# Where the modulation panels stand in a shared weight ring: from fours in projections and branches to pairs in attentions and norms

## The chip, the cores and the metric

The kernel runs on 1 core of one Trainium2 chip. The metric is the device time of one execution in microseconds (us); lower is better. The engines have short names: PE (TensorE, matrix products), PEld (its weight loads), DVE (VectorE), ACT (ScalarE), POOL (GpSimd) and SP (SyncE, which issues the DMAs here).

## The reference

Two transformer blocks run one after the other on 256 tokens (the first also carries 256 context tokens), each with two layers, all in float32. The change touches only the first block:

```python
for l in range(DEPTH):                                    # DEPTH = 2
    mod_x = (silu(c) @ w_ada[l] + b_ada[l])               # 6 * 1024 columns
    mod_c = (silu(c_ctx) @ w_ada[l] + b_ada[l])
    sh1, sc1, g1, sh2, sc2, g2 = split(mod_x, 6)          # and the same of mod_c
    h = layer_norm(x) * (1 + sc1) + sh1
    p = h @ w_in[l]                                       # keys, values, queries, gates, Fourier input
    mix = gates * [fourier(..) @ w_fo, attend_m(..) @ w_mo, attend_g(..) @ w_go] @ w_o
    x = layer_norm(alpha * x + g1 * mix)
    h2 = layer_norm(x) * (1 + sc2) + sh2
    x = layer_norm(alpha * x + g2 * (relu(h2 @ w1) ** 2 @ w2))
```

The vectors c and c_ctx do not depend on the layers, so the product with `w_ada` (1024 x 6144 a layer, 48 MB in both) may be computed at any moment before its sixth is used.

## The kernel before

**One ring of weights.** Every weight reaches the chip as a panel of 1 MB (128 partitions x 2048 floats) in a ring of four slots. SP issues the loads in the order in which PE uses the panels. The load of panel n waits on `panel_begun` until the first matmul of panel n-3 is done, since from then on the slot of panel n-4 is free. So at most three panels are loaded or on their way while one is in use.

**Two kinds of panels.** A dense panel is split in two before use: ACT copies it with rounding into `ring_hi` (one instruction, L1466, in a function called `split`), and POOL subtracts that from the panel into `ring_lo`, which the profile calls `ring_r` (four instructions, L1446). PE waits for `lo_ready` of the slot (L751) and runs 48 matmuls (three products for each of 16 tile pairs; L783). A modulation panel (`w_ada`, 256 columns) isn't split: PE waits only for its landing. One call of `modulate()` on PE takes two such panels, a group: 2 x 8 matmuls against `silu_c` (the profile shows 32 records), then, for the group before, four small matmuls which turn its rows into columns (8 records, reading `hid_v` or `p_cmp`). ACT copies the rows out of PSUM (L1487), and DVE adds the bias (L2070). The 48 modulation panels are 24 groups; the first 4 groups stand ahead of everything, since layer 0 needs sh1 and sc1 at once.

**All orders are written by hand.** Each engine's program is a straight list, and each engine executes it in order. ACT's `split` of a dense panel stands in general two panels ahead of PE's use. Since POOL and the counters treated four slots as a unit, modulation panels stood in fours. The other 20 groups stand in layer 0: 4 in `project` (2 after its fourth dense panel and 2 at its end), 6 in the attention of kind m, 6 in that of kind g, and 4 in `branches` (2 after each of its two halves of six dense panels). Layer 1 has none.

**The norms.** `norm` sums x over its 1024 channels by 8 matmuls with ones, DVE centres, ACT squares, PE sums the squares, ACT takes the root, DVE the reciprocal and scales; in a norm with modulation ACT then applies scale and shift and rounds, and DVE makes the low part. After `mix_out` two norms follow each other, then the MLP's first panel; after the MLP one norm ends layer 0 and one opens layer 1.

**Attention.** A unit is one pair of heads on 128 queries. In step u PE computes the scores of unit u, then whatever else is placed there, then transposes the probabilities of unit u-1 (L810), then multiplies those of u-2 with the values. In kind m some steps also hold parts of the Fourier transform.

## Time and profile before

| What | Value |
|---|---|
| Median of three runs | 3257.94 us (3250.87 to 3266.14) |
| The profiled execution | 3254.99 us, its span 3253.2 us |
| PE busy | 2943.5 us, 90% of the span |
| First block and the start, 0 to about 1775 us | PE busy 1558.32 us |
| Second block, about 1775 us on | PE busy 1385.22 us of 1478.00 us |
| Granted TensorE clock, whole run | 0.947 |

PE leads in busy time everywhere, so the question for any stretch is what PE waits for in it, and what work PE does there that could stand elsewhere. In rows of the timeline the first number is the start in us, the second the duration, and the bracket at the end gives the idle time of the engine just before and what ended it.

### The profile page before, as it was taken

What the parts mean: (1) busy time and instruction counts of PE and PEld (TensorE: products, weight loads), DVE (VectorE), ACT (ScalarE), POOL (GpSimd) and SP (SyncE); (2) the same over time, 40 slices, a digit from 0 to 9 for tenths busy, and PEclk for the clock granted to TensorE, in tenths of its full rate; (3) what the DMA queues carried; (4) which work ended last, traced back from release to release, by engine and by line L of the source; (5) the groups of instructions that cost most, each with busy time, mean ns of one, the idle gap of its engine ahead of it and who ended that gap; (6) DMA issues with size and microseconds to landing.
All of it is one profiled execution on the core that took longest, in us unless ns stands there. A gap on an engine that the chain in (4) does not pass through costs nothing.

```text
span 3253.2 us, 49328 instructions
## 1 busy us (share of the span) xinstructions
PE 2943.5 (90%) x20273; PEld 2605.7 (80%) x20273; DVE 889.1 (27%) x1620; ACT 1244.7 (38%) x1672; POOL 1784.8 (55%) x1380
## 2 busy tenths in 40 slices
PE   5799888887999979889897999899998999899998
PEld 4576656674887847679897999889998998889998
DVE  1223233125112252333334212144211212144211
ACT  1423443223223233553443434454433434455432
POOL 1220214341545404247585887855887887756885
PEclk8889999989999989999999999999999999999999
DMA  7433325341322313135443556533454556534453
GB/s 222 116 92 112 95 98 156 122 129 30 100 90 91 97 32 91 53 104 156 130 170 128 161 176 169 169 117 117 156 182 156 169 180 171 169 104 130 156 181 117
DMA packets 397385, 422.60 MB, mean 130 GB/s; under 512 B 74550, under 2 KB 367406, under 8 KB 396919
## 3 DMA queue, kind: packets, MB, share of 16 engines
q1 hardware_dynamic: 397208, 420.06, 41.5%
q8 instruction: 134, 2.20, 0.3%
q14 instruction: 43, 0.35, 0.0%
HBM read 418.96 MB, written 3.16 MB: 130 GB/s over the span
## 4 chain that ended last, share of the span: by engine, by line
PE 82%; DVE 5%; POOL 5%; DMA 3%; ACT 3%; issue 2%; SPq 1%; DVEq 0%; POOLq 0%; ACTq 0%
PE ps L783 64%; PE ps L767 16%; POOL ring_r L1446 5%; PE ps L810 2%; ACT ring_hi L1466 1%; DVE arena L2092 1%; DMA ring<-in_w_in 1%; DVE stat L2205 1%; DMA ring<-in_w_ada 1%; DVE arena L2219 1%; DMA arena<-in_bucket_of_block 0%; PE ps L824 0%; DVE arena L2371 0%; DMA ring<-in_ffn_w_gate 0%; DMA ring<-in_w_branch_gla 0%
## 5 line engine op out<-in xcount | busy, mean ns | idle before, releaser
L1446 POOL TENSOR_TENSOR ring_r<-ring,ring_hi 128x512 fp32r<-128x512 f32 x1376 | 1784.6, 1333 | 1439.0 <-ACT ring_hi L1466 1437.0
L783 PE MATMUL ps<-hT_r,ring_hi 128*128 128x256 f32 (+1 forms) x6304 | 1178.7, 310 | 101.5 <-DVE hT_r L2384 36.6
L783 PEld LDWEIGHTS ps<-hT_r,ring_hi 128*128 128x128 f32 x6304 | 956.3, 197 | 169.3 <-issue 44.5
L1466 ACT ACTIVATE ring_hi<-ring 128x2048 fp32r<-128x2048 f32 x344 | 658.0, 1914 | 568.8 <-DMA ring<-in_ffn_w_down 136.3
L783 PE MATMUL ps<-hT_r,ring_r 128*128 128x256 f32 (+1 forms) x3152 | 712.6, 308 | 0.0
L783 PE MATMUL ps<-arena_r,ring_hi 128*128 128x256 f32 (+1 forms) x3792 | 641.8, 311 | 27.0 <-DVE arena_r L2293 9.5
L783 PEld LDWEIGHTS ps<-arena_r,ring_hi 128*128 128x128 f32 x3792 | 542.1, 190 | 74.1 <-issue 23.8
L783 PEld LDWEIGHTS ps<-hT_r,ring_r 128*128 128x128 f32 x3152 | 523.9, 196 | 24.7
L783 PE MATMUL ps<-arena_r,ring_r 128*128 128x256 f32 (+1 forms) x1896 | 358.4, 310 | 0.0
L783 PEld LDWEIGHTS ps<-arena_r,ring_r 128*128 128x128 f32 x1896 | 284.2, 190 | 20.8
L767 PE MATMUL ps<-arena 128*64 128x128 f32 (+9 forms) x1616 | 201.0, 366 | 24.6 <-DVE arena L2181 11.9
L767 PEld LDWEIGHTS ps<-arena 128*64 128x64 f32 (+4 forms) x1616 | 125.8, 174 | 70.4 <-issue 51.4
L2400 DVE TENSOR_TENSOR arena<-arena,ps 128x256 f32 (+1 forms) x88 | 33.1, 418 | 420.9 <-ACT arena L1812 420.9
L767 PE MATMUL ps<-arena,const 128*128 128x256 f32 (+3 forms) x348 | 105.3, 458 | 35.1 <-ACT arena L1494 17.1
L2350 DVE TENSOR_TENSOR arena_r<-arena,arena_r 128x512 fp32r<-128x512 f32 (+1 forms) x64 | 84.3, 1340 | 161.1 <-ACT arena_r L1755 161.1
L810 PE MATMUL ps<-const,arena 128*128 128x128 f32 x480 | 75.9, 307 | 53.8 <-DVE arena L2219 39.2
L767 PEld LDWEIGHTS ps<-arena,const 128*128 128x128 f32 (+2 forms) x348 | 66.1, 200 | 70.7 <-issue 47.4
L767 PE MATMUL ps<-ring_hi,hT_r 128*128 128x128 f32 (+2 forms) x640 | 114.6, 279 | 4.1 <-POOL ring_r L1446 2.5
L810 PEld LDWEIGHTS ps<-const,arena 128*128 128x128 f32 x480 | 63.1, 159 | 68.4 <-DVE arena L2219 50.7
L1632 ACT ACTIVATE arena<-ps,stat,rstd 128x512 f32<-128x512 f32 (+1 forms) x96 | 67.0, 702 | 123.3 <-DVE stat L2209 123.3
L1812 ACT ACTIVATE arena<-ps 128x256 f32<-128x256 f32 x88 | 29.1, 383 | 182.9 <-PE ps L783 182.9
L767 PEld LDWEIGHTS ps<-ring_hi,hT_r 128*128 128x128 f32 (+1 forms) x640 | 93.2, 175 | 6.0 <-POOL ring_r L1446 3.1
(215 smaller groups left out, 1954.7 us busy)
## 6 DMA issues: line engine op xcount, KB each, us to landing
ring<-in_w_in SPq DMA_DIRECT2D x82, 1024.0 KB
ring<-in_w SPq DMA_DIRECT2D x64, 1024.0 KB
ring<-in_w_ada SPq DMA_DIRECT2D x48, 1024.0 KB
ring<-in_ffn_w_up SPq DMA_DIRECT2D x44, 1024.0 KB
ring<-in_ffn_w_gate SPq DMA_DIRECT2D x44, 1024.0 KB
ring<-in_ffn_w_down SPq DMA_DIRECT2D x44, 1024.0 KB
ring<-in_w_in SPq DMA_DIRECT2D x48, 256.0 KB
ring<-in_w_o SPq DMA_DIRECT2D x8, 1024.0 KB
```

Of the source, the lines that this page charges most:

```text
L767: mm = pe.matmul(o, lhsT, rhs, start=start and j == 0, stop=stop and j == len(passes) - 1, skip_group_check=True)
L783: last[t] = pe.matmul(o, lhsT, rhs, start=start and j == 0, stop=stop and j == n - 1, skip_group_check=True)
L810: return pe.transpose(o, src, ident)
L1446: ins = pool.tensor_tensor(k.ring_lo[s][:, part], k.ring[s][:, part], k.ring_hi[s][:, part], ALU.subtract)
L1466: act.activation(k.ring_hi[s][:, :], k.ring[s][:, :], ACT.Copy).then_inc(k.hi_ready[s], 1)
L1632: act.activation(prob[:, buf, a, 0:n], ps[:, b, 0:n], ACT.Exp, bias=k.stat[:, 8 * buf + a:8 * buf + a + 1], scale=rstd_cq[:, tt:tt + 1] if ...
L1812: act.activation(area(SILU2, 2, 2, SEQ)[:, j % 2, m, :], ps[:, b, 0:SEQ], ACT.Silu).then_inc(k.bank_read[b], 1)
L2092: dve.reciprocal(std, std).then_inc(S["dve_step"], 1)
L2205: ins = dve.tensor_reduce(nmax[:, a:a + 1], ps[:, b, 0:n], AX, ALU.max, negate=True)
L2219: ins = dve.tensor_scalar(p, p, rsum[:, a:a + 1], None, ALU.mult)
L2350: dve.tensor_tensor(hid_lo[:, kt, :], hid[:, kt, :], hid_hi[:, kt % HID_SLOTS, :], ALU.subtract) \
L2400: dve.tensor_tensor(x[:, m, :], area(SILU2, 2, 2, SEQ)[:, j % 2, m, :], ps[:, b, 0:SEQ], ALU.mult) \
```

## The change

The change lets the two kinds of panels mix at any place of the ring. A string `RING` says of each panel of the first block whether it is a modulation panel (a) or dense (d). The counters of splits are kept for each slot, ACT's `split` skips modulation panels, and POOL's program, which was one loop, is written out for the first block. On that basis the 20 groups are placed anew: 6 in attention m of layer 0, 2 in attention g of layer 0, 3 in the norm after `mix_out`, 1 in the second norm, 3 in the norm after the MLP, 1 in the first norm of layer 1, 3 in attention m and 1 in attention g of layer 1. `project` and `branches` hold none. DVE adds the bias of groups in norms only after the norm. `mix_out` and the MLP of layer 0 no longer split the last two panels ahead; these splits now stand in the norm (one ahead of the scaling, one behind).

```diff
+RING = "a" * ADA_FIRST + "d" * 10 + "a" * 12 + "dddd" + "aa" + "dd" + "aa" + "d" * 16 + "a" * 8 + "d" * 32 + "a" * 8 \
+    + "d" * 10 + "a" * 6 + "dddd" + "aa" + "d" * 18 + "d" * 32
...
-QUADS_M, QUADS_G = (4, 6, 8, 10, 12, 14), (7, 8, 13, 14, 15, 16)
-AHEAD_M, AHEAD_G = (13, 15), (9, 10, 16, 17)
+MODS_M, MODS_G, MODS_LAST = ((4, 6, 8, 10, 12, 14), (2, 4, 6)), ((8, 13), (4,)), (14, 5)
+AHEAD_M, AHEAD_G = ((13, 15), (6, 7)), ((7, 9, 14, 15), (4, 5))
...
@@ SP: the order of the loads
-                    if c == 0 and l == 0:
-                        modulations(8, 4)
                 cols(416, 256)
-                if l == 0:
-                    modulations(12, 4)
...
-                if l == 0:
-                    modulations(16, 12)
+                modulations(*((8, 12) if l == 0 else (40, 6)))
                 for n in (0, 512):
                     gates(0, n)
-                if l == 0:
-                    modulations(28, 4)
+                modulations(20 if l == 0 else 46, 2)
                 for n in (0, 512):
                     out_of("w_fo", n)
                 if l == 0:
-                    modulations(32, 8)
+                    modulations(22, 2)
...
-                    if l == 0:
-                        modulations(40 + n // 128, 4)
                 for j in range(4):
                     s = slot()
                     load(s, [(at(s, 0, KD, 256), rows(W["w_o"][lay])[:, :, 256 * j:256 * j + 256])])
+                if l == 0:
+                    modulations(24, 8)
...
             mix_and_mlp(0)
+            modulations(32, 8)
             project(1)
...
@@ PE
-            def norm(cols, added):
+            def norm(cols, added, fill=(0, 0)):
...
                 mm.then_inc(k.bank_done[b], 1)
+                for _ in range(fill[0]):
+                    modulate()
                 sq = area(SQ, KD, TOK)
...
                 mm.then_inc(k.bank_done[b], 1)
+                for _ in range(fill[1]):
+                    modulate()
...
-                norm(slice(0, TOK), x_moved if l == 0 else None)
+                norm(slice(0, TOK), x_moved if l == 0 else None, (l, 0))
+                if l == 1:
+                    modulated_last()
...
-                norm(cols, last_results())
-                norm(cols, None)
+                fill = l == 0
+                norm(cols, last_results(), (1, 2) if fill else (0, 0))
+                norm(cols, None, (fill, 0))
+                if fill:
+                    modulated_last()
                 mlp(l, cols)
-                norm(cols, last_results())
+                norm(cols, last_results(), (1, 2) if fill else (0, 0))
...
@@ ACT
             def split():
 
+                while T.kind(1) == "a":
+                    T.whole_panel()
                 s, rounds, _ = T.panel()
...
+                for _ in range(fill[1]):
+                    modulate()
+                if last:
+                    modulated_last()
+                    split()
                 if affine:
```

Three places show how this moves instructions. First ACT in `project` of layer 0: the L1565/L1568 pairs take a query tile out of PSUM, L1466 is a split and L1487 the copy of a group's rows. Before:

```order
L1565 ACTIVATE arena<-ps 128x512
L1568 ACTIVATE arena<-ps,vecT 128x512
L1487 ACTIVATE hid_v<-ps 128x512
L1466 ACTIVATE ring0_hi<-ring0 128x2048
L1487 ACTIVATE p_cmp<-ps 128x512
L1466 ACTIVATE ring1_hi<-ring1 128x2048
L1565 ACTIVATE arena<-ps 128x512
```

The same place of the changed kernel (L1583/L1586 are the tiles, L1489 is the split):

```order
L1489 ACTIVATE ring1_hi<-ring1 128x2048
L1583 ACTIVATE arena<-ps 128x512
L1586 ACTIVATE arena<-ps,vecT 128x512
L1583 ACTIVATE arena<-ps 128x512
L1586 ACTIVATE arena<-ps,vecT 128x512
L1489 ACTIVATE ring2_hi<-ring2 128x2048
```

The copies of group rows are gone from between the query tiles, and each split stands ahead of the tiles before it.

Second, PE in the two norms after `mix_out` of layer 0. The changed kernel (xT,const are the sums of x, arena,const those of the squares, ring,silu_c one modulation panel, the 128x2 rows turn a group; before, only the four rows with 128x512 stood here):

```order
L774 MATMUL ps<-xT,const 128x512 x8
L774 MATMUL ps<-ring0,silu_c 32x256 x8
L774 MATMUL ps<-ring1,silu_c 32x256 x8
L774 MATMUL ps<-arena,const 128x512 x8
L774 MATMUL ps<-ring2,silu_c 32x256 x8
L774 MATMUL ps<-ring3,silu_c 32x256 x8
L774 MATMUL ps<-const,hid_v 128x2 x4
L774 MATMUL ps<-ring0,silu_c 32x256 x8
L774 MATMUL ps<-ring1,silu_c 32x256 x8
L774 MATMUL ps<-const,p_cmp 128x2 x4
L774 MATMUL ps<-xT,const 128x512 x8
L774 MATMUL ps<-ring2,silu_c 32x256 x8
```

One group now stands between the sums of x and of the squares, and two behind the squares, ahead of the next norm's sums.

Third, ACT from the second norm's root (L1498) to the MLP. Before (four splits stand in `mix_out`, ahead of the norms; the last two of them are those of the first two MLP panels):

```order
L1494 ACTIVATE arena<-arena 128x512 x8
L1498 ACTIVATE arena<-ps,const 128x512
L1505 ACTIVATE arena<-arena,mods 128x256 x4
L1510 ACTIVATE hT_r<-arena 128x512
...
L1505 ACTIVATE arena<-arena,mods 128x256 x2
L1510 ACTIVATE hT_r<-arena 128x512 x2
L1466 ACTIVATE ring2_hi<-ring2 128x2048
```

The changed kernel:

```order
L1518 ACTIVATE arena<-ps,const 128x512
L1489 ACTIVATE ring0_hi<-ring0 128x2048
L1530 ACTIVATE arena<-arena,mods 128x256 x4
L1535 ACTIVATE hT_r<-arena 128x512
...
L1535 ACTIVATE hT_r<-arena 128x512 x2
L1489 ACTIVATE ring1_hi<-ring1 128x2048
L1489 ACTIVATE ring2_hi<-ring2 128x2048
```

The splits of the MLP's first two panels (ring0, ring1) moved from ahead of the norms to one place between root and scaling and one behind the rounding. The first norm of layer 1 has the same form.

## Rows read from the trace of the kernel before

**Rows 1.** The page, part 1: busy time of each engine.

```profile
PE 2943.5 (90%) x20273; PEld 2605.7 (80%) x20273; DVE 889.1 (27%) x1620; ACT 1244.7 (38%) x1672; POOL 1784.8 (55%) x1380
```

**Rows 2.** Stretches: start:end, length, busy time by engine, granted clock, DMA share, GB/s.

```profile
140.10:157.70 17.60, 6.48 (x73) 3.79 (x73) 0.17 (x1) 6.84 (x8) 5.00 (x5) 0.67 0.90 238
187.50:197.30 9.80, 7.54 (x82) 4.70 (x81) 0.17 (x1) 2.10 (x3) 0.00 (x0) 0.82 0.88 275
197.30:212.90 15.60, 15.60 (x72) 13.19 (x72) 3.52 (x2) 4.56 (x5) 9.88 (x8) 0.61 0.42 98
598.90:614.70 15.80, 5.87 (x80) 3.61 (x80) 2.92 (x6) 6.23 (x5) 4.99 (x5) 0.75 0.81 265
614.70:683.60 68.90, 68.89 (x292) 55.95 (x295) 9.68 (x13) 11.18 (x12) 26.39 (x20) 0.96 0.31 92
683.60:702.20 18.60, 9.48 (x89) 6.45 (x89) 7.93 (x12) 9.36 (x9) 7.39 (x6) 0.64 0.70 226
748.70:797.50 48.80, 29.76 (x66) 12.32 (x64) 30.84 (x45) 15.84 (x27) 0.00 (x0) 0.93 0.00 0
```

**Rows 3.** Timeline of PE in layer 0's projection, around the first modulation groups.

```profile
140.03 2.80 PE L767 MATMUL ps<-ring,silu_c 128*32 128x256 f32 x48
146.15 1.94 PE L767 MATMUL ps<-ring,silu_c 128*32 128x256 f32 x16 [3.33 <-DMA ring<-in_w_ada]
...
157.68 2.07 PE L783 MATMUL ps<-hT_r,ring_hi 128*128 128x512 f32 x4 [7.80 <-POOL ring_r L1446]
```

**Rows 4.** The chain that ended last, same place: start, duration, what.

```profile
152.70 4.94 POOL ring_r L1446 x4
...
157.68 13.69 PE ps L783 x48
```

**Rows 5.** Timeline of PE in layer 0's attention g.

```profile
446.94 1.94 PE L767 MATMUL ps<-ring,silu_c 128*32 128x256 f32 x32
448.80 1.05 PE L767 MATMUL ps<-const,hid_v 128*128 128x2 f32 x8
...
454.56 1.09 PE L810 MATMUL ps<-const,arena 128*128 128x128 f32 x8 [2.56 <-DVE arena L2219]
...
462.21 2.07 PE L783 MATMUL ps<-arena_r,ring_hi 128*128 128x512 f32 x4 [4.91 <-POOL ring_r L1446]
...
511.14 1.93 PE L767 MATMUL ps<-ring,silu_c 128*32 128x256 f32 x32
...
530.45 2.07 PE L783 MATMUL ps<-hT_r,ring_hi 128*128 128x512 f32 x4 [4.57 <-POOL ring_r L1446]
```

**Rows 6.** Timeline of DVE between layer 0's branches and `mix_out`.

```profile
685.65 0.69 DVE L2283 TENSOR_TENSOR arena<-arena 128x512 f32<-128x512 f32 x1
...
699.84 2.24 DVE L2293 TENSOR_TENSOR arena_r<-arena,arena_r 128x1024 fp32r<-128x1024 f32 x1
```

**Rows 7.** Timelines of PE, ACT and POOL: layer 0's two norms and the MLP's start.

```profile
758.06 7.11 PE L767 MATMUL ps<-arena,const 128*128 128x512 f32 x16 [2.33 <-ACT arena L1494]
771.21 8.49 PE L767 MATMUL ps<-xT,const 128*128 128x512 f32 x16 [6.04 <-DVE xT L2106]
...
797.47 2.04 PE L783 MATMUL ps<-hT_r,ring_hi 128*128 128x512 f32 x4 [8.33 <-DVE hT_r L2100]
...
806.06 1.91 ACT L1466 ACTIVATE ring_hi<-ring 128x2048 fp32r<-128x2048 f32 x1
810.28 1.09 ACT L1745 ACTIVATE arena<-ps 128x512 f32<-128x512 f32 x2 [2.31 <-PE ps L783]
...
808.05 11.03 POOL L1446 TENSOR_TENSOR ring_r<-ring,ring_hi 128x512 fp32r<-128x512 f32 x8 [68.67 <-ACT ring_hi L1466]
```

**Rows 8.** Timeline of PE in layer 1's attention m, steps 4 and 6.

```profile
1333.52 2.86 PE L767 MATMUL ps<-const,arena 128*128 128x256 f32 x12
...
1350.44 1.09 PE L810 MATMUL ps<-const,arena 128*128 128x128 f32 x8 [0.64 <-DVE arena L2219]
```

**Rows 9.** The line L2283 of DVE, all of it: duration ns min/median/max, forms.

```profile
L2283 DVE TENSOR_TENSOR arena<-arena x32: 424/942/1229, 560.8 to 1511.0; 128x512 f32<-128x512 f32 x16, 128x256 f32<-128x256 f32 x16
```

More of the change, by code:

```diff
@@ L210, in whole_panel, with kind, split_rounds @@
         n = self.next("panel")
+        assert self.kind() == "a"
         slot = (self.count["panel"] - 1) % SLOTS
         return slot, self.value("panel", SLOTS - 1, SLOTS), n
-    def split_rounds(self):
-        return self.value("split", SLOTS - 1, SLOTS)
+    def kind(self, ahead=0):
+        j = self.count.get("panel", 0) - 1 + ahead
+        return RING[j] if j < PANELS_1 else "d"
+    def split_rounds(self, slot):
+        return self.value(f"split{slot}")
     @contextmanager
@@ L222, in loop @@
         tiles = per.pop("tiles", 0)
-        if "panel" in per and not per.pop("whole", False):
-            per["split"] = per["panel"]
+        for slot in range(SLOTS if "panel" in per else 0):
+            per[f"split{slot}"] = per["panel"] // SLOTS
         for j in range(tiles):
@@ L1476, in _ @@
             skip(KD)
-            def whole():
-                for _ in range(2):
-                    T.whole_panel()
             def modulation(group):
@@ L1495, in norm @@
                         .then_inc(S["squared"], 1)
+                for _ in range(fill[0]):
+                    modulate()
                 b, v = T.take()
@@ L1521, in modulate, with modulated_last @@
                 ada["turn"] = True
-            def whole_panels(quads):
-                for _ in range(2 * quads):
-                    whole()
+            def modulated_last():
+                skip(1)
+                ada["turn"] = False
             def project(l, cols):
@@ L1700, in branches @@
                         for j in range(3):
-                            last_two = l == 0 and g == 2 and j >= 1
-                            if not last_two:
-                                split()
+                            split()
                             if j == 2:
@@ L1773, in _ @@
                 halves, mod = (0, 1) if l == 0 else (1,), l * MODS
-                norm(plain, slice(0, TOK), modulated(mod + SC1, mod + SH1, (0, 1)))
+                fill = l == 0
+                norm(plain, slice(0, TOK), modulated(mod + SC1, mod + SH1, (0, 1)), (l, 0), not fill)
+                if l == 1:
+                    split()
                 project(l, cols)
@@ L2079, in scales, with norm @@
                 dve.wait_ge(S["dve_step"], T.next("dve_step"))
-            def norm(dst, cols, affine, ready):
+            def norm(dst, cols, affine, ready, fill=(0, 0), last=False):
                 n = cols.stop - cols.start
@@ L2088, in norm @@
                 dve.wait_ge(*k.moved(T.last()))
+                for _ in range(fill[0]):
+                    modulate()
                 for kt in range(KD):
                     dve.tensor_tensor(dst[:, kt, cols], k.xT[:, kt, cols], mean, ALU.subtract).then_inc(S["centred"], 1)
-                dve.wait_ge(*k.moved(skip(1)))
+                deviation = skip(1)
+                for _ in range(fill[1]):
+                    modulate()
+                if last:
+                    modulate(rows=False)
+                dve.wait_ge(*k.moved(deviation))
                 dve.reciprocal(std, std).then_inc(S["dve_step"], 1)
@@ L2308, in _ @@
                 if group >= 1:
-                    modulation(group - 1)
-            modulation(group)
+                    modulation(group - 1, *T.take())
+            modulation(group, *T.take())
             scales((SC1,))
@@ L2316, in _ @@
                 mod = l * MODS
-                norm(plain, slice(0, TOK), None, "h_ready")
+                fill = l == 0
+                norm(plain, slice(0, TOK), None, "h_ready", (l, 0), not fill)
                 project(l, cols)
@@ L2329, in _ @@
                 dve.wait_ge(*k.moved(T.last()))
-                norm(k.xT, cols, gained("ln1", l), "x_ready")
-                norm(plain, cols, None, "h_ready")
+                norm(k.xT, cols, gained("ln1", l), "x_ready", (1, 2) if fill else (0, 0))
+                norm(plain, cols, None, "h_ready", (fill, 0), fill)
+                if fill:
+                    scales((MODS + SC1,))
                 x = k.xT[:, :, cols]
```

166 lines of the change are left out of this document (70 added, 96 removed).

## The prediction, made before the changed kernel ran

> **What bounds the kernel now.** I read the page first, for the busy shares: PE 90%, POOL 55%, nothing else over 40% [rows 1]. PE also leads in every stretch that I cut with the windows. So a gain needs either less idle time of PE in layer 0 of the first block, or PE work moved from stretches where PE is full to stretches where it waits. Then I went through PE's timeline for idle times of a microsecond and more, and took the windows of the places where modulation groups stand [rows 2]. The reader is to see two things there. Where groups stand between dense panels, PE is busy for 6.48 us of 17.6, 7.54 of 9.8, 5.87 of 15.8 and 9.48 of 18.6. And the clock in them is 0.64 to 0.82, against 0.96 beside them. The reason is in the timeline: the first three panels of the four are there, the fourth is waited for (its load starts when the first is begun at 140.03 and it lands at 146.15, so a load takes 6.1 us when PE asks for it last), and the next dense panel, loaded later still, then needs its split and POOL's 4.94 us, so that PE starts again only at 157.68 [rows 3, 4]. Four light panels empty a ring of four, and the refill with the split is exposed.
>
> **The cost of a group.** 1.94 us for its two panels and 1.05 for turning the group before, 2.99 together at full clock [rows 5]; the 20 groups are 60 us of PE. A group that follows a finished series has none to turn and costs 1.94.
>
> **The cost of a restart.** A dense panel at full clock, p, and the loss of a restart, r: 13.69 = p + r [rows 4], and six panels with one restart take 68.9 = 6p + r [rows 2]. So p = 11.04, r = 2.65 us. The granted clock falls to the lower level (1.2 of 2.4 GHz) after waits like these, and the first matmuls after 157.68 take 2.07 us for four.
>
> **Gains, step by step.**
> (1) Projection of layer 0: the stretches of 17.6 and 9.8 us vanish, and one restart: 30.0. Nothing else waits there: p is twice POOL's 5 us for a panel and more than a load.
> (2) The sums that follow (197.3 to 212.9) ran at clock 0.61; 15.6 x 0.61 = 9.5 us at full clock [rows 2]. They came out of a group with waits; now they follow dense work, whose stretches have 0.96. Between 0 and 6.1; I take 5, since most of the sums' instructions are tiny and the clock may fall within them.
> (3) Attention g of layer 0. The wait of 4.91 us on POOL at 462.21 and its restart go (7.6), because the splits for w_fo stand in steps 7 and 9 and only two light panels precede. The removed groups themselves bring next to nothing: between scores and transposes PE waits 2.56 us anyway for DVE [rows 5], and a group fills that. At the end the last scores are at 511.14, and dense work starts at 530.45 [rows 5]. Without groups there the remaining steps are the 2.56 us wait, two pairs of transposes and three products with the values, at 1.1 us each, and one more step of ACT and DVE of about the length of that wait: 2.6 + 5.5 + 0.6 = 8.7, to about 519.8. That is 10.6 less, and the restart shrinks (2). Sum 20.2. Bounds: 7.6 if the end stays DMA-bound, 21.
> (4) Branches: the stretch of 15.8 us and its restart go (18.4). Behind the last branch panel 18.6 us become what the chain to `mix_out` needs: DVE's last sum ends at 686.34, 2.7 us after 683.6, ACT rounds (not longer than DVE's 2.24 for the same tile), DVE splits in 2.24 [rows 6]: 6 to 7, I take 6.2. Gain 12.4. Sum 30.9.
> Together 30.0 + 5 + 20.2 + 30.9 = 86.1 us.
>
> **Costs, step by step.**
> (5) The 8 groups in norms. The gap between the sums is 2.33 us [rows 7]: 1.94 fits, 2.99 costs 0.65. Two of the four have a group to turn: 1.3. The two groups behind the squares take 5.98 against a wait of 6.04 [rows 7], if their panels are there. The ring holds three when the norm begins; the fourth, fifth and sixth are loaded as the first, second and third are begun. The sixth is asked for at about 765.3 and is here at 771.4 by the 6.1 us above, so the next sums start near 772.4 and not at 771.21. They take 7.1 us at full clock but were stretched to 8.49 by DVE's pace, ending at 779.7: 772.4 + 7.1 = 779.5, no loss. Bounds 0 and, if loads under way together take twice 6.1, 6 us at each of the two places. I take 0.
> (6) The second split. Before, two panels were ready when the MLP began. Now the second is split behind ACT's rounding, from 806.06 + 0.65 on: ACT 1.91, POOL 11.03 / 2 = 5.5 [rows 7], ready at 814.1. The first panel is done at 810.28 + 0.65 (ACT reads it then). PE waits about 3.3 us, here and again at the projection of layer 1: 6.6. The third panel follows on POOL 5.5 us later, while PE needs 11, so it is not late.
> (7) The first split now has POOL at work while DVE scales the first tiles. DVE's additions from SBUF range from 0.42 to 1.23 us [rows 9], 0.69 for 512 columns with POOL at rest [rows 6]. Three such instructions lie on the way to the first h tile: 0 to 1.6 us at each of two places; I take 1 each, 2.
> The Trainium skill, "SBUF — State Buffer", section "Who interferes with whom", says that a DVE instruction with two SBUF inputs and a GpSimd one that reads SBUF share one port pair as an exclusive lock, held for a whole instruction. By that rule the place could cost one POOL instruction per DVE one, near the upper bound; the maximum of 1.23 agrees, as 0.69 and a part of a wait.
> (8) Layer 1's attentions take four groups. In m, step 2 has room; in step 4 the Fourier products of 2.86 us already fill the wait, so a group costs 2.9; in step 6 0.64 us is left, so 2.3 [rows 8]. In g 2.99 stands against 2.56: 0.4. Sum 5.6, bounds 1 and 12.
> Costs 1.3 + 6.6 + 2 + 5.6 = 15.5.
>
> **The sum.** The profiled execution took 3254.99 us, 3 us less than the median of 3257.94. 86.1 - 15.5 = 70.6 less gives 3184 against the profiled one, and 3187 for the median.
>
> **The rivals.**
> *Late refills in the norms.* PE's queue is in order: a group that waits for its panel holds the sums behind it, and these head the chain of the whole norm. For it speaks that eight panels are used in 30 us where 3 are in the ring. Against it: nothing else is loaded there (share 0.00 from 748.7 to 797.5), and the stretch of 17.6 us moved 238 GB/s, that is four panels [rows 2]. Each late panel costs up to 6.1; with 12 us at each of the two pairs of norms, and the second MLP panel later by the same slip, 30 us go back: 3217.
> *The bubbles move along.* The waits on POOL behind light panels could remain behind pairs, in attention g and at its end. Then of (3) only 7.6 is left or less and the layer 1 attention costs its 12: about 20 back, 3207. Against it: a pair leaves two dense panels in the ring, and their splits stand ahead.
> *More than summed.* Groups between the sums keep PE at work in the norms, so that the clock is still high when dense work comes, which now restarts at 797.47 with four matmuls in 2.04 us [rows 7]. Four restarts of 2.65 less would be 10.6: 3176. The Trainium skill, "TensorE: Matmul & The Clock Gate", Part 1, says that the throttled state is the default and activity releases it. Against it here: only one turn of 1.05 us falls into the last wait of 8.33.
> *Slower.* ACT's split in the norm stands ahead of the scaling. If the panel lands late, ACT holds h, and all behind it. Now nothing loads then, and this panel is asked for only when the sixth light panel is begun. It would have to be 36 us late at both places to eat 70.6 and 44 to be called slower; a load takes 6.1.
> *It doesn't do what it says.* POOL's program written out could run slower than the loop (its instructions must be fetched), and be the one PE waits for: POOL had 5 of 11 us to do, so it would have to double. Then the dense panels of layer 1, with half the tokens and so about p / 2, would be POOL's. That would leave 3230 to 3260.
>
> **How the numbers follow.** Chances: the forecast (3175 to 3200) 0.62, late refills 0.12, bubbles that move along 0.10, more than summed 0.10, POOL 0.04, slower 0.02. Range 3170 to 3218: from the third rival less some spread of runs (they differed by 15 us) to the first. A measurement of this kernel can tell about 0.5%, 16 us, from no change. Faster by over 0.5% holds all but the last two: 0.94; same 0.04, slower 0.02.
>
> **What would show it.** Projection of layer 0 without idle time of PE and about 30 us shorter; the sums behind it at a clock near 1; no L1446 wait in attention g; the branches in two times 66 us without a break and `mix_out` some 6 us behind. In the norms the 32x256 matmuls inside the old idle times, and the pair of norms with its start of dense work not over 3 us longer than its 48.8 [rows 2]. A wait of 3 us on POOL at the second panel of the MLP and of layer 1's projection. Layer 1's attention m some 5 us longer. I am wrong if PE waits on `w_ada` loads for more than 10 us in the norms, or if POOL's waits return in layer 1.

## The result and the profile after

The changed kernel takes 3208.67 us in the median of four runs (3207.76 to 3210.62), the kernel before 3260.78 us in four runs beside it (3250.87 to 3266.14). The ratio is 0.9844, with a 95% interval of 0.9819 to 0.987: faster by 1.6%, and 52.1 us less where the prediction had worked out 70.6. That is inside its range of 3170 to 3218, but outside the 3175 to 3200 to which it gave a chance of 0.62. The two profiled executions, which the stages below go by, have spans of 3253.2 and 3206.0 us: 47.2 less.

First the page of the changed kernel, part 1:

```profile
PE 2939.2 (92%) x20273; PEld 2603.9 (81%) x20273; DVE 899.4 (28%) x1620; ACT 1244.0 (39%) x1672; POOL 1780.7 (56%) x1380
```

PE works as long as before (2943.5 in [rows 1]), so nearly all that was gained is idle time. Where it went is read from windows cut at PE's own marks: the first dense panel of a stage, the first sums, the first scores. Of the kernel before, in the columns of [rows 2]: layer 0's projection, its attention g, the part of that up to the first `w_fo` panel, its end from the last scores beside a dense panel, the branches, the first half of the MLP, then layer 1's projection and attention m:

```profile
94.70:197.30 102.60, 89.22 (x513) 71.59 (x513) 10.92 (x18) 30.32 (x47) 19.94 (x16) 0.88 0.45 129
376.60:530.50 153.90, 128.38 (x879) 93.80 (x877) 50.84 (x124) 70.86 (x131) 27.26 (x21) 0.94 0.38 123
376.60:462.20 85.60, 71.16 (x418) 52.29 (x416) 25.96 (x73) 44.76 (x88) 15.16 (x12) 0.95 0.30 99
495.80:530.50 34.70, 26.20 (x310) 17.71 (x308) 15.46 (x32) 19.87 (x31) 7.11 (x5) 0.92 0.75 243
530.50:702.20 171.70, 152.65 (x744) 121.64 (x745) 35.81 (x44) 40.03 (x38) 69.21 (x50) 0.91 0.40 123
797.50:977.00 179.50, 176.12 (x769) 145.38 (x769) 31.15 (x47) 56.41 (x69) 81.48 (x64) 0.99 0.29 94
1206.90:1296.70 89.80, 82.52 (x506) 73.25 (x506) 30.41 (x48) 38.45 (x62) 40.85 (x32) 0.94 0.38 94
1296.70:1366.20 69.50, 60.13 (x380) 40.09 (x380) 25.51 (x56) 28.29 (x58) 10.11 (x8) 0.91 0.10 31
```

The same stretches of the changed kernel, with the sums behind the projection as its second row and the two norms as its seventh; these two answer to the rows 197.30 and 748.70 of [rows 2]:

```profile
97.30:169.50 72.20, 72.20 (x361) 61.41 (x362) 10.61 (x16) 30.67 (x44) 30.18 (x24) 0.98 0.37 88
169.50:182.50 13.00, 13.00 (x72) 11.56 (x70) 3.35 (x1) 1.97 (x3) 0.00 (x0) 0.73 0.00 1
344.50:496.60 152.10, 128.68 (x726) 94.56 (x724) 49.45 (x119) 65.08 (x124) 30.11 (x24) 0.87 0.21 70
344.50:430.30 85.80, 73.89 (x378) 52.98 (x376) 22.77 (x66) 43.66 (x83) 16.26 (x13) 0.89 0.23 74
463.90:496.60 32.70, 23.76 (x197) 17.96 (x195) 13.21 (x28) 14.25 (x25) 10.05 (x8) 0.74 0.20 65
496.60:634.10 137.50, 132.22 (x578) 108.11 (x577) 36.38 (x38) 39.65 (x34) 65.75 (x48) 1.00 0.32 92
681.50:735.90 54.40, 42.82 (x226) 20.87 (x224) 34.11 (x47) 19.84 (x31) 5.83 (x4) 0.87 0.49 155
735.90:922.90 187.00, 178.77 (x769) 147.00 (x769) 31.69 (x50) 58.28 (x70) 86.81 (x68) 0.97 0.28 90
1156.30:1250.80 94.50, 85.19 (x506) 74.92 (x506) 30.66 (x50) 40.42 (x63) 45.68 (x36) 0.92 0.36 89
1250.80:1326.60 75.80, 68.86 (x492) 46.56 (x492) 25.59 (x58) 29.78 (x61) 10.23 (x8) 0.87 0.35 112
```

The reader is to see: the projection is 30.4 us shorter and has no idle time left, the branches 34.2 shorter at a clock of 1.00. But attention g is only 1.8 us shorter, although it has four groups (some 12 us of PE) less to do and its wait on POOL ahead of `w_fo` is gone. Its clock fell from 0.94 to 0.87, to 0.74 at its end, and PE is busy for 128.68 us where it was for 128.38: 153 records fewer, in the same busy time. The costs stand in the norms (+5.6), the MLP (+7.5), layer 1's projection (+4.7) and its attention m (+6.3).

PE in attention g of the changed kernel. L817 transposes the probabilities, and the row of 477.96 holds the last scores:

```profile
426.60 1.09 PE L817 MATMUL ps<-const,arena 128*128 128x128 f32 x8 [2.63 <-DVE arena L2221]
...
476.06 1.97 PE L817 MATMUL ps<-const,arena 128*128 128x128 f32 x8 [1.55 <-DVE arena L2221]
...
477.96 2.77 PE L774 MATMUL ps<-arena 128*64 128x128 f32 x20
484.22 1.97 PE L817 MATMUL ps<-const,arena 128*128 128x128 f32 x8 [3.49 <-DVE arena L2221]
...
491.30 1.97 PE L817 MATMUL ps<-const,arena 128*128 128x128 f32 x8 [3.21 <-DVE arena L2221]
```

The same transposes (eight records) take 1.09 us and then 1.97, near the ratio of the two levels of the clock (2.4 and 1.2 GHz), and two of the three waits on DVE at the end are longer than the 2.56 us of [rows 5]. DVE in the same place (L2221 scales the probabilities, two tiles), and POOL's splits of the first two branch panels under it:

```profile
475.13 0.88 DVE L2221 TENSOR_SCALAR arena<-arena,stat 128x512 f32<-128x512 f32 x2
...
482.42 1.74 DVE L2221 TENSOR_SCALAR arena<-arena,stat 128x512 f32<-128x512 f32 x2
...
488.67 2.58 DVE L2221 TENSOR_SCALAR arena<-arena,stat 128x512 f32<-128x512 f32 x2
```

```profile
478.56 4.93 POOL L1456 TENSOR_TENSOR ring_r<-ring,ring_hi 128x512 fp32r<-128x512 f32 x4 [44.46 <-ACT ring_hi L1489]
485.85 5.12 POOL L1456 TENSOR_TENSOR ring_r<-ring,ring_hi 128x512 fp32r<-128x512 f32 x4 [2.37 <-ACT ring_hi L1489]
```

With POOL at rest the pair of L2221 takes 0.88 us, beside it 1.74 and 2.58.

Behind the projection PE is never idle, and yet the clock falls. These are the 64 products with one column, which end the sums, and the first dense products behind them:

```profile
172.06 10.54 PE L774 MATMUL ps<-const,arena 128*128 128x1 f32 x64
182.46 2.05 PE L790 MATMUL ps<-arena_r,ring_hi 128*128 128x512 f32 x4
```

The norms and the MLP's start on PE:

```profile
697.90 1.93 PE L774 MATMUL ps<-ring,silu_c 128*32 128x256 f32 x32
...
703.90 1.37 PE L774 MATMUL ps<-ring,silu_c 128*32 128x256 f32 x16 [2.07 <-DMA ring<-in_w_ada]
705.19 1.87 PE L774 MATMUL ps<-const,p_cmp 128*128 128x2 f32 x8
706.92 9.31 PE L774 MATMUL ps<-xT,const 128*128 128x512 f32 x16
...
735.88 2.04 PE L790 MATMUL ps<-hT_r,ring_hi 128*128 128x512 f32 x4 [9.03 <-DVE hT_r L2107]
...
753.21 2.08 PE L790 MATMUL ps<-hT_r,ring_hi 128*128 128x512 f32 x4 [4.85 <-POOL ring_r L1456]
```

The row of 697.90 begins the third modulation panel of the norms, at which the load of the sixth is asked for. The sixth is waited for (2.07 us), its group is followed by a turn at the lower clock (1.87 for 1.05), the sums take 9.31 where [rows 7] has 8.49, and the second MLP panel costs a wait of 4.85 on POOL and a restart (2.08 for its first four products). DVE's three scalings ahead of the MLP, beside the first split (POOL 728.66 to 734.49):

```profile
730.21 4.83 DVE L2104 TENSOR_TENSOR arena<-arena 128x512 f32<-128x512 f32 x3
...
735.65 0.69 DVE L2104 TENSOR_TENSOR arena<-arena 128x512 f32<-128x512 f32 x1
```

That is 1.61 us for one beside POOL, and 0.69 for one without.

### The profile page after: what moved, and what is told of

Same layout as the page of the kernel before. It is cut to its first block, busy times and chain, and to the rows that moved or that the text cites. A ratio compares the mean times of both kernels' runs of the same rounds, so it can differ in the third digit from the quotient of the medians.

```text
span 3206.0 us, 49208 instructions
## 1 busy us (share of the span) xinstructions
PE 2939.2 (92%) x20273; PEld 2603.9 (81%) x20273; DVE 899.4 (28%) x1620; ACT 1244.0 (39%) x1672; POOL 1780.7 (56%) x1380
## 4 chain that ended last, share of the span: by engine, by line
PE 83%; DVE 6%; POOL 4%; ACT 2%; DMA 2%; issue 2%; SPq 0%; DVEq 0%; POOLq 0%; ACTq 0%
PE ps L790 64%; PE ps L774 16%; POOL ring_r L1456 4%; PE ps L817 2%; DVE arena L2221 1%; DMA ring<-in_w_ada 1%; DVE stat L2207 1%; ACT ring_hi L1489 1%; DVE arena L2099 0%; ACT arena L1530 0%; PE ps L831 0%; DMA arena<-in_bucket_of_block 0%; DVE arena L2376 0%; DVE arena L2104 0%; DMA ring<-in_ffn_w_gate 0%
## 5 line engine op out<-in xcount | busy, mean ns | idle before, releaser
L1456 POOL TENSOR_TENSOR ring_r<-ring,ring_hi 128x512 fp32r<-128x512 f32 x1376 | 1780.5, 1331 | 1395.9 <-ACT ring_hi L1489 1394.9
L1489 ACT ACTIVATE ring_hi<-ring 128x2048 fp32r<-128x2048 f32 x344 | 657.8, 1914 | 502.8 <-DMA ring<-in_ffn_w_down 136.6
L774 PE MATMUL ps<-arena 128*64 128x128 f32 (+9 forms) x1616 | 205.8, 374 | 21.0 <-DVE arena L2184 11.9
L817 PE MATMUL ps<-const,arena 128*128 128x128 f32 x480 | 79.4, 316 | 63.4 <-DVE arena L2221 48.8
L817 PEld LDWEIGHTS ps<-const,arena 128*128 128x128 f32 x480 | 65.9, 164 | 76.9 <-DVE arena L2221 59.0
L774 PE MATMUL ps<-arena,const 128*128 128x256 f32 (+3 forms) x348 | 103.1, 451 | 24.7 <-ACT arena L1792 11.9
```

The source lines that it names most:

```text
L774: mm = pe.matmul(o, lhsT, rhs, start=start and j == 0, stop=stop and j == len(passes) - 1, skip_group_check=True)
L817: return pe.transpose(o, src, ident)
L1456: ins = pool.tensor_tensor(k.ring_lo[s][:, part], k.ring[s][:, part], k.ring_hi[s][:, part], ALU.subtract)
L1489: act.activation(k.ring_hi[s][:, :], k.ring[s][:, :], ACT.Copy).then_inc(k.hi_ready[s], 1)
```

## The experiments

The question was where 18 of the 20.2 us of term (3) went. *Theory A*: the waits that the removed groups no longer fill bring the clock to its lower level, and all work in and behind them takes longer. *Theory B*: the chain of scores, DVE, ACT and POOL sets the steps, and the clock only fills idle time. Others size the costs and rule out rivals. All kernels but `pool_written` are the changed one with the edit shown, and all ran five times or more beside the kernel before. The first four ran on one chip, where the kernel before stood at 3252.08 us (3250.62 to 3266.75, nine runs) and the changed one did not run. So a few us of their medians against 3208.67 are not certain, and their weight lies in the stages. The next four ran on one other chip, and one of them is the changed kernel again.

**Filler in three steps** (`g_filler`). Four products of constants that nothing reads, ahead of PE's wait for the probabilities:

```diff
+                            if a == 0 and l == 0 and kind == "g" and u in (14, 15, 16):
+                                for _ in range(4):
+                                    pe.matmul(ps[:, b, 0:256], ident, dft_d, start=True, stop=True, skip_group_check=True)
+                            if a == 0:
+                                pe.wait_ge(S["prob_ready"], T.next("prob_ready"))
```

> The changed kernel, with four matmuls of 256 columns without use ahead of the transposes in steps 14, 15 and 16 of layer 0's attention g, where PE waits for DVE. Theory A (the clock: the stretch from the last group of that attention to the branches took 29.7 us at a clock of 0.71, since the groups that used to fill PE's waits are gone): more PE work, yet the stretch gets 3 to 6 us shorter, clock over 0.85, median 3203 to 3206 against 3208.7. Theory B (POOL's splits slow DVE's L2221 from 0.88 to 1.74 and 2.58 us, and ACT's splits stand ahead of its copies): the stretch stays within 1 us of 29.7 or grows by up to 2.

Measured: 3212.48 us (3206.38 to 3215.37), ratio 0.9867 [0.9843, 0.9891], not faster than the changed kernel. The stretch from the last group to the branches is 26.9 us (466.6 to 493.5) for 29.7, at a clock of 0.87 for 0.71, and one of its three sets of transposes is still cold (at the lower clock, 1.97 us), behind a wait of 2.79. The clock is where theory A had it, the 2.8 us are just short of its 3 to 6, and the total does not show them. Alone it decided nothing: the clock was low in the steps ahead of these too.

**Splits one step earlier** (`g_early`).

```diff
-AHEAD_M, AHEAD_G = ((13, 15), (6, 7)), ((7, 9, 14, 15), (4, 5))
+AHEAD_M, AHEAD_G = ((13, 15), (6, 7)), ((7, 9, 13, 14), (4, 5))
```

> The changed kernel, with the splits of the branches' first two panels in steps 13 and 14 of layer 0's attention g, instead of 14 and 15. Theory B (POOL beside DVE): the last two L2221 pairs are back at 0.88 us for an instruction's pair as before, the stretch of 29.7 us gets 2 to 4 shorter, median 3205 to 3207. Theory A (clock): nothing or below 1 us, and the clock stays near 0.71.

Measured: 3210.41 us (3201.68 to 3212.38), ratio 0.9855 [0.983, 0.9879]. The same stretch takes 27.3 us at a clock of 0.81: the waits there are 3.40, 2.64 and 1.52 instead of 1.55, 3.49 and 3.21. The long ones moved one step forward with POOL's work. So POOL beside DVE is a part of the end, of about 2.4 us as theory B said, and the median does not show it.

**Both splits ahead of the scaling in the norms** (`two_splits`): ACT and POOL start the MLP's second panel before the h tiles, not behind them.

```diff
                 for _ in range(fill[1]):
                     modulate()
                 if last:
                     modulated_last()
                     split()
+                    split()
...
-                if l == 1:
-                    split()
...
-                if fill:
-                    split()
```

> The changed kernel, with both splits of the first two dense panels behind the norms standing together between root and scaling (before: one there, one behind the rounding), ahead of the MLP and of layer 1's projection. Theory: PE's waits of 4.85 and 2.02 us on POOL at the second panel and the restarts at the lower clock go: 4.85 + 2.65 and 2.02 + 2.65, less 0.5 each for ACT's second split ahead of the scaling: about 11 less, 3198. Rival: POOL then works beside DVE's scaling twice as long (DVE's three scalings took 4.84 beside POOL and 1.90 without), the first dense matmul comes 2 to 4 us later at both places, and the gain is 3 to 6: 3203 to 3206.

Measured: 3203.22 us (3200.77 to 3206.75), ratio 0.9844 [0.9821, 0.9866]; by the ratio no better than the changed kernel, by the median 5.5 us under it. The first half of the MLP takes 181.5 us for 187.0, layer 1's projection 91.7 for 94.5: 8.3 us of the 12.2 that the second split cost are back in these stages. But the norms ahead of them grew, from 54.4 to 55.3 us and from 52.6 (55.2 when the changed kernel ran again) to 56.7, since POOL's work on both panels now lies under the scaling. That is what the rival said, and its 3203 to 3206 came, not the 3198 of the theory. DVE:

```profile
725.08 4.84 DVE L2101 TENSOR_TENSOR arena<-arena 128x512 f32<-128x512 f32 x3
729.93 1.67 DVE L2104 TENSOR_TENSOR hT_r<-arena,hT_r 128x512 fp32r<-128x512 f32 x1
731.52 1.76 DVE L2101 TENSOR_TENSOR arena<-arena 128x512 f32<-128x512 f32 x1
```

**The norms' groups as one, one, one** (`norm_spread`) in place of one, two, none, so that no place needs four panels at once.

```diff
-                norm(cols, last_results(), (1, 2) if fill else (0, 0))
-                norm(cols, None, (fill, 0))
+                norm(cols, last_results(), (1, 1) if fill else (0, 0))
+                norm(cols, None, (fill, fill))
```

> The changed kernel, with the groups in norms as 1 between the sums and 1 behind the squares in each of the four norms, instead of 1 and 2, then 1 and 0. Theory of the late refill: the waits of 2.07 and 1.95 us for the sixth panel go, and the slow sums behind them (9.31 and 8.73 us instead of 8.5): the pairs of norms take 51 and 50.5 instead of 54.2 and 52.5, 5 us less: 3204. If the group in the last wait (9.03 us) also keeps the clock up, the first dense panel starts at full clock, 2.65 less at each place: 3199. Rival: the dense panels are now asked for later, the second split waits for its panel, and PE's wait behind the first dense panel grows by what the norms gain: 3208.

Measured: 3205.5 us (3203.18 to 3208.27), ratio 0.9846 [0.9823, 0.9869]. No wait for a panel is left in the norms. The second norm's sums start 13.15 us after the first norm's squares, as in the kernel before, where the changed kernel has 16.05, and they take 8.80 us for 9.31: 3.4 us less. But the two norms take 52.2 us for 54.4, only 2.2 less, and the pair that ends layer 0 takes 52.9 for 52.6. ACT copies the third group's rows ahead of its split, so that POOL comes last at the first dense panel, and this still starts at the lower clock:

```profile
731.17 2.07 PE L790 MATMUL ps<-hT_r,ring_hi 128*128 128x512 f32 x4 [7.29 <-POOL ring_r L1456]
```

So the group that stood in front of the sums was 3.4 us of the 5.6, and its new place gives 1.2 of them back. Of the two further parts of the expectation neither came: the group in the last wait did not keep the clock up, and the wait behind the first dense panel became shorter (3.90 us for 4.85), not longer.

**The changed kernel again** (`after_again`), without an edit.

> The changed kernel unaltered, so that the four kernels of this call have it on their own chip. If what I ascribe to the clock's phase is right, the same instructions take different times: attention g of layer 0 took 152.09, 146.55 and 152.14 us in three kernels that have it unaltered, and the norms that end layer 0 took 52.6, 56.7 and 52.9. I expect one of those values, the stages of dense work alone (branches 137.5, MLP's second half 180.8) within 0.3 us of before, and a median of 3205 to 3212.

Measured: 3208.43 us (3207.28 to 3215.14), ratio 0.985 [0.9835, 0.9864]. Attention g took 146.7 us in its profile, not 152.1; attention m 133.6 for 130.8, the norms that end layer 0 55.2 for 52.6; the branches 137.5 in both. The stretch from the last group to the branches is the same to 0.1 us, so the difference in attention g lies ahead of it. Here is its window, to be held against 344.50:496.60 above:

```profile
348.90:495.60 146.70, 122.92 (x726) 91.40 (x724) 49.27 (x119) 64.85 (x124) 30.17 (x24) 0.90 0.22 72
```

The same 726 records take 5.8 us less of PE at 0.90 than at 0.87. In stretches with waits the clock differs from run to run; in the branches it does not, and in the dense projection of layer 0 little (72.2 and 72.9 us). This is why one profile's stage is good to about 5 us there and to 0.1 in the branches.

**Filler in every waiting step of attention g** (`g_full`).

```diff
-                            if a == 0 and l == 0 and kind == "g" and u in (14, 15, 16):
+                            if a == 0 and l == 0 and kind == "g" and u in (1, 3, 5, 7, 9, 11, 14, 15, 16):
```

> Four unused 128x256 products stand ahead of PE's wait for the probabilities in every step of layer 0's attention g that waits (1, 3, 5, 7, 9, 11, 14, 15, 16), about 1.7 us each at full clock in waits of 1.8 to 2.6 us. Theory A (the lost 18 us of term 3 are mostly a lower clock, which the waits bring): the clock of the stage goes from 0.87 to 0.97 or more, the dense panels in it to 11.2 from 11.9 and 12.6, transposes to 1.07, the stage from 152 to 141 to 145 us, the whole to 3199 to 3203. Theory B (the chain through ACT, DVE and POOL sets the steps and the clock only fills their idle time): the stage stays at 149 to 154, the whole at 3207 to 3212.

Measured: 3201.32 us (3200.55 to 3202.67), ratio 0.9828 [0.9813, 0.9842], 7.1 us less than the changed kernel beside it, with no range in common. The stage, its part up to the `w_fo` panel, and its end:

```profile
342.00:480.80 138.80, 130.71 (x798) 97.73 (x796) 51.77 (x119) 64.64 (x124) 30.57 (x24) 0.99 0.24 76
342.00:420.30 78.30, 74.70 (x419) 55.65 (x417) 22.85 (x66) 42.74 (x82) 15.32 (x13) 1.00 0.25 81
451.60:480.80 29.20, 25.35 (x221) 18.57 (x219) 14.67 (x28) 14.17 (x25) 10.24 (x8) 0.94 0.23 73
```

The stage is 13.3 us shorter than in the changed kernel's first profile and 7.9 shorter than in its second, with 72 records more to do. The part up to `w_fo` takes 78.3 us for 85.8: 7.3 under the kernel before, where the prediction's first part of term (3) said 7.6. (The part held two groups before and holds one now, so the two numbers are near in part by luck.) Theory A holds, B falls for this part: PE is idle for 3.6 us of it where it was for 11.9, and its clock is 1.00 for 0.89. The four products take 2.0 us, not 1.7. Beside it stands what the Trainium skill says ("TensorE: Matmul & The Clock Gate", Part 1): the throttled state is the default and activity releases the throttle. By that rule work of no use can make a kernel faster, and this trace agrees: 0.87 without the products, 0.99 with them.

**The three placements together** (`three`): `g_early`, `two_splits` and `norm_spread`.

> Three edits together: the splits of attention g in steps 13 and 14 in place of 14 and 15, both splits of the norms ahead of the scaling, and the groups in the norms as one, one and one in place of one, two and none. If their effects by stages are real and add (attention g -6 to -8, MLP and projection of layer 1 -8.3, norms -2.2), the median is 3190 to 3195. If only what the medians showed adds (+1.7, -5.5 and -3.2), it is 3200 to 3204, and the difference is the phase of the clock, which an edit shifts at will.

Measured: 3197.42 us (3194.43 to 3201.44), ratio 0.9813 [0.9799, 0.9828]; 11.0 under the changed kernel beside it. Between the two forecasts (3190 to 3195, 3200 to 3204): the medians of the three alone add to 7.0 (-5.5, -3.2 and +1.7), the stages in the expectation to 16.5 and more. The stages do not simply add: the norms take 54.9 and 56.2 us here, so that the 2.2 us that the spread groups gained there do not show beside the two splits, and attention g takes 149.6.

**POOL written out in the kernel before** (`pool_written`): its loop unrolled for 24 rounds of four panels (`low` is the old body of the loop), all else as it was.

```diff
-            with pool.Fori(0, (PANELS_1 - ADA + LAYERS * PANELS_2) // SLOTS) as i:
+            written = 24
+            for i in range(written):
                 for s in range(SLOTS):
...
+                    low(s, i + 1)
+            with pool.Fori(0, (PANELS_1 - ADA + LAYERS * PANELS_2) // SLOTS - written) as i:
+                for s in range(SLOTS):
+                    low(s, i + 1 + written)
```

> The kernel before, with POOL's loop written out for its first 96 panels and looped for the rest, all else as before. Tests my rival that the written-out program is slower by itself. Theory: it costs nothing, as POOL has 5 of 11 us to do: the median of the kernel before within 5 us, POOL's four instructions for a panel 4.94 us as before. Rival: instruction fetch makes POOL late, with new waits on it in projection and branches, over 3265 us.

Measured: 3259.19 us (3251.15 to 3266.68, 12 runs) against 3257.72; ratio 1.0002 [0.9989, 1.0014]. POOL's line over the whole run, this kernel and then the kernel before (count, busy time, mean ns, idle time by releaser):

```profile
L1445 POOL TENSOR_TENSOR ring_r<-ring,ring_hi 128x512 fp32r<-128x512 f32 x1376 | 1784.0, 1330 | 1448.1 <-ACT ring_hi L1473 1446.5
```

```profile
L1446 POOL TENSOR_TENSOR ring_r<-ring,ring_hi 128x512 fp32r<-128x512 f32 x1376 | 1784.6, 1333 | 1439.0 <-ACT ring_hi L1466 1437.0
```

The rival that a written-out program runs slower falls. PE's program is that of the kernel before, so this profile is also a second one of it, and its attention g takes 159.0 us where the first has 153.9 (attention m 129.8 for 131.8).

**Placements and filler** (`three_full`): `three` with the products of `g_full`. This run and the next ran on a third chip, with the kernel before at 3258.4 us.

> The three edits of the run before together with the four unused products ahead of every waiting step of layer 0's attention g. If the products' gain of 7 us is the clock's and independent of where the splits stand, attention g falls from 149.6 to 138 to 141 us and the median from 3197 to 3188 to 3192. If the edits share one gain (the splits in steps 13 and 14 were already part of it), the median stays at 3194 to 3198.

Measured: 3193.08 us (3190.67 to 3199.54), ratio 0.9805 [0.979, 0.982]. Attention g takes 137.2 us, just under the 138 to 141 of the first theory, but the median lies between the two forecasts (3188 to 3192, 3194 to 3198). It is 4.3 below that of `three`, which ran on another chip, and the ranges of the two overlap. At the end no transposes are cold any more, and PE (L1051 is the filler) goes from the end of the last scores (469.61 + 2.15, in one row with the products ahead of them) to the branches in 10.2 us. From the last group (457.51) on it is 24.5 us at a clock of 1.00, 5.2 less than the 29.7 of the changed kernel, and `g_filler` and `g_early` had 2.8 and 2.4:

```profile
469.61 2.15 PE L774 MATMUL ps<-arena 128*64 128x128 f32 x20
471.70 1.99 PE L1051 MATMUL ps<-const 128*128 128x256 f32 x8
475.23 1.09 PE L817 MATMUL ps<-const,arena 128*128 128x128 f32 x8 [1.54 <-DVE arena L2222]
...
479.11 1.04 PE L817 MATMUL ps<-const,arena 128*128 128x128 f32 x8
...
481.97 1.19 PE L790 MATMUL ps<-hT_r,ring_hi 128*128 128x512 f32 x4
```

**Filler in the other attentions too** (`fill_more`): the same products in `u in {"m0": (13, 15, 16), "g0": ..., "m1": (7, 8), "g1": (5, 7)}`.

> As the run beside it, and the same four products also in the waits of the other attentions: steps 13, 15, 16 of m in layer 0 (waits 2.63, 2.63, 3.38), steps 7 and 8 of m in layer 1 (2.84, 2.85, transposes at 1.97) and steps 5 and 7 of g in layer 1 (4.51, 2.56). If the clock is what a wait costs beyond itself everywhere, attention m of layer 0 loses 2 to 4 us, that of layer 1 3 to 5, attention g of layer 1 1 to 3: the median is 6 to 10 us below the run beside it, 3180 to 3185. Rival: the products stand in the way in places where the wait is shorter than they are, and the median is within 3 us of the run beside it.

Measured: 3184.52 us (3182.28 to 3186.29), ratio 0.9772 [0.9759, 0.9785], 8.6 below `three_full` beside it, as the theory said (6 to 10), with no range in common, and 24 below the changed kernel on another chip: the best version here. Attention m of layer 0, then m and g of layer 1:

```profile
210.70:340.40 129.70, 119.43 (x845) 80.57 (x845) 45.02 (x117) 48.29 (x116) 10.28 (x8) 0.95 0.36 114
1228.00:1301.30 73.30, 69.63 (x508) 46.86 (x508) 26.13 (x58) 29.68 (x61) 10.25 (x8) 0.93 0.36 116
1301.30:1373.00 71.70, 67.74 (x575) 57.08 (x573) 30.81 (x66) 47.30 (x75) 30.36 (x24) 0.98 0.37 118
```

Against `three_full` these are 1.3, 2.7 and 1.0 us less, 5.0 together, each at or just under the low end of its forecast (2 to 4, 3 to 5, 1 to 3). The other 3.6 I can't place: the two profiles differ by more than that in the second block alone, which is the same code (1458.5 and 1453.0).

## Why the prediction came out as it did

The direction and the range were right, and the order of the steps: idle time behind light panels was the thing to gain. The forecast itself was 22 us too low. The measured time is near the 3207 of the rival whose bubbles move along, but by chance, as that mechanism did not appear. By its own steps:

- **(1) Projection, 30.0:** 30.4. Right.
- **(2) The sums behind it, 5:** 2.6, and the heads after them 0.7. The clock there rose from 0.61 to 0.73 only (0.78 in the repeat), where I had said near 1. The first sums, behind dense work at 0.98, run at 1.00, and the 64 tiny products behind them (10.54 us, 11.45 before) at 0.66, although PE is not idle, so I now take it that they, and not the group ahead, hold the clock down (argued from the rows, not tried). I had named that doubt and taken the value near the bound.
- **(3) Attention g, 20.2:** 1.8 in the profile, 7.2 in the repeat. This is the term that failed: 18.4 of the 23.4 between 70.6 and 47.2. Since the kernel before has 153.9 and 159.0 us in two profiles, the size is only good to some us; both attentions of layer 0 together gained 2.8 to 8.5. Its first mechanism was right: the wait on POOL of 4.91 is gone, and with the clock held up the part ahead of `w_fo` loses 7.3 us of the 7.6, and the end takes 10.2 us from the last scores where I had 8.7. What failed is the sentence that the removed groups "bring next to nothing", because a wait stands where each stood. The wait costs more than itself: without the group PE idles 1.2 to 3.5 us in a step, and the work in and behind it runs at the lower level. Filling these waits gave back 13.3 us (7.9 against the repeat). In the changed kernel the end took 15.9 us from the last scores (477.96 + 2.77, to 496.6). Of the 7.2 over my 8.7, 5.7 are not there with filler and earlier splits. My sum for the end was also wrong in itself: it has 0.6 us for one more step of ACT and DVE that it calls about as long as the 2.6 us wait, and with 2.6 it is 10.7.
- **(4) Branches, 30.9:** 34.2. All twelve panels in 132.2 us without a break, as said, and 5.3 to `mix_out` where I took 6.2. Most of the rest is the restart at 530.45, which went too: it lies in this stage, and I had booked it under (3) with 2.
- **(5), (7) The norms:** 5.6 in the first pair and 2.0 in the second (4.6 in the repeat), where I had 1.65 each. The load was not the mistake. The third panel is begun at 697.90 and the sixth is here at 703.90, 6.0 us later where I had 6.1, and the wait of 2.07 us is the one that my times contain. The slip is in what stands behind it. I let the sums start 1.0 us after the landing and run at full clock (7.1). They start 3.0 us after it, because a group is turned there (1.05, which I left out) and panel and turn run slower behind the wait, and they take 9.31. DVE does not set their pace here: its last tile is ready 5.5 us before they end, 1.8 in the kernel before, and the granted clock from 703.9 to 716.2 is 0.72. That is 3.7 us of the 5.6, and again a wait that costs more than itself. Most of the rest is the scaling. POOL beside DVE cost about 1 us for each 128x512 instruction that it overlaps, (4.83 - 3 x 0.69) = 2.8 for the three, for which I had 1 and a bound of 1.6. One POOL instruction for each of them would be 3 x 1.33 = 4.0, so my sentence that this is near the upper bound was wrong. Not all of the 2.8 arrives: from the root (ACT, 726.10) to the dense work are 9.8 us for 8.3.
- **(6) The second split, 6.6:** 12.2. The wait was 4.85 us in place of 3.3 at the MLP (2.02 at layer 1's projection): the first panel took 12.5 us, not 13.5, and the second was ready 17.3 us after the start, not 16.6. Behind each wait came a restart of 2.65, which I had measured myself and not charged. Wait and restart together are 7.5 and 4.67, the whole of what the two stages grew by in this profile (7.5 and 4.7; 7.4 and 6.4 in the repeat).
- **(8) Layer 1's attentions, 5.6:** 5.2 (6.3 and -1.1). Right, in its sum.
- **Rivals and signs:** bubbles did not move along (no wait on POOL in attention g). PE waited for a late panel in both pairs of norms, 2.07 and 1.95 us, far from the 12 of the rival. That light panels in the norms keep the clock up did not come: 0.87 in them for 0.93, and the dense panel, behind 9.03 us of idle time, still begins with 2.04 us for four products. POOL written out costs nothing. Two of the signs that I had named failed: the clock in the sums (0.73), and the norms (5.6 us longer, not at most 3). So the gain came out smaller than forecast by 17.1 on the side of the gains and 9.5 on that of the costs, less the 3 below.

The steps add: 30.4 + 2.6 + 1.8 + 34.2 = 69.0 gained, 7.6 + 12.2 + 5.2 = 25.0 lost, 44.0 in all. The 3 us up to 47.2 are the sum of all other stages, the largest of them the second block (-4.9) and the start (+2.6), which the change leaves alone and which differ by as much between two runs of one kernel.

What stays open: `g_filler` and `g_early` each gave 2.8 and 2.4 us at the end of attention g and 5.2 together, but neither shows in a median by itself. POOL beside DVE makes a wait longer, and a wait comes with a lower clock, so a part of its price may be the clock's; no run separates the two further. What the tiny products do to the clock was not tried.

## What to carry to other kernels

Work that fills an engine's wait is not free to remove: count what its absence does to the clock of TensorE in and behind the wait, and where nothing useful fits, a few products that nobody reads are worth trying (here 7 us of the kernel's time with one stage filled and 8.6 more with three others, of which the stages show 5). Charge a restart (2.65 us here) with a wait that an edit adds (here 2.0 to 4.9 us), as well as with those it takes away. Read a stage with waits from more than one profile. And place GpSimd's work where VectorE rests: under the work that heads a chain, VectorE's 128x512 instructions on SBUF took about 1 us more each.

## What the runs showed of the hardware

- The same program in two profiled runs: 152.1 and 146.7 us for the same 726 records of attention g, at a granted clock of 0.87 and 0.90, while the dense branches took 137.5 us in both. What clock a stretch with waits gets is in part a matter of the run.
- 64 products with one column, behind dense work and without idle time, were granted a clock of 0.66, and the four dense products behind them took 2.05 us where they take 1.07 at full clock.
- VectorE beside GpSimd, both on SBUF: 1.67 and 1.76 us for an instruction that takes 0.69 alone, and 1.74 and 2.58 for a pair of 0.88. A reduction that VectorE makes from PSUM took 1.29 us for two with GpSimd at work and without. The Trainium skill ("SBUF — State Buffer", "Who interferes with whom") gives an exclusive lock of a shared port pair. This trace agrees in the size: the 1 us more is near the 1.3 us that one of POOL's instructions takes (mean 1331 ns). In `three_full` the pair under POOL's work (463.12 to 468.25) takes 2.74 us, and the next, behind POOL's work (469.23 to 474.17), 0.88. The small instruction between them reads two tiles in SBUF and takes 0.16 us elsewhere. Here it took 0.99 and ended at 474.18, when POOL's work did:

```profile
465.80 2.74 DVE L2222 TENSOR_SCALAR arena<-arena,stat 128x512 f32<-128x512 f32 x2
...
473.19 0.99 DVE L2212 TENSOR_TENSOR stat<-stat,rstd 128x2 f32<-128x2 f32 x1
...
474.29 0.88 DVE L2222 TENSOR_SCALAR arena<-arena,stat 128x512 f32<-128x512 f32 x2
```

- 24 rounds of a loop written out on GpSimd: 1330 ns for an instruction, 1333 in the loop.
